# Triangle inversion in a one-core decoder-trunk kernel: the second head's products of the last four steps go to the opposite half of the partitions, and the heads get PSUM banks of their own

## The chip, the core and the metric

The kernel runs on one core of a Trainium2 chip (trn2). The core has TensorE (PE, matrix products into PSUM; its weight loads are listed apart as PEld), VectorE (DVE), ScalarE (ACT), GpSimd (POOL) and SyncE (SP, which issues most DMAs). TensorE's clock has two levels, 1.2 and 2.4 GHz, and the profile states which share of full speed was granted. The metric is the device time of one execution in microseconds (us), and lower is better.

## What is computed

One inference step of a two-layer decoder trunk: layer 0 is an RWKV-7 time mixing with a mixture of experts behind it, layer 1 a sparse attention with another mixture of experts, for a prompt of 512 tokens and 8 samples of 4 tokens. The change lies in the time mixing alone. Its recurrence runs over 16 heads of 64 channels, in f32:

```python
def wkv7_scan(r, w, k, v, a, b, s0):
    def step(s, inp):
        r_t, w_t, k_t, v_t, a_t, b_t = inp
        sa = jnp.einsum('bhij,bhj->bhi', s, a_t)
        s = s * w_t[:, :, None, :] + sa[..., None] * b_t[:, :, None, :] + v_t[..., None] * k_t[:, :, None, :]
        return s, jnp.einsum('bhij,bhj->bhi', s, r_t)
```

The kernel doesn't step through the tokens of the prompt. It cuts them into 8 chunks of 64 tokens. Within a chunk the dependence of one token on the others is a unit triangular 64x64 matrix, which has to be inverted for each head and chunk. The chunks' states are then joined one after the other.

## The kernel before

**Rounds and steps.** The heads are worked in 8 pairs (a pair is two heads, h = 0 and 1). `pe_rwkv`, `act_rwkv` and `dve_rwkv` each write out the same loop: a round per pair, a round has 8 steps s = 0 to 7, and a round works on four pairs at once: pair `a` is prepared (prep), pair `b` is inverted, pair `c` has its states computed (post, chunk), and pair `d` is finished (tail). Each engine works its own list strictly in the order of this code, and waits on semaphores for the others. On TensorE a step is the inversion of `b`, then post of `c`, then the prep of `a`, a small product for the samples, and a second prep part. So what the inversion leaves to TensorE in a step comes before everything else in that step.

**The inversion.** A pair has 16 matrices of 64x64: 2 heads, 4 values of q, and 2 values of r (chunk 2q + r). `UNITS4` lists them as (q, h, r), r fastest. An SBUF tile such as `Tt` holds the matrices with r = 0 on partitions 0 to 63 and those with r = 1 on partitions 64 to 127. `hs(r)` is that half. Steps 0 to 3 build the inverse of the 16x16 blocks by squaring. Steps 4 to 7 do two doublings (16 to 32, 32 to 64), each in two steps:
- step 4 or 6: TensorE transposes T (L958, a product with the identity) and forms L times T (L959), 2 x 16 products of 64x64x64. ScalarE copies the transposes from PSUM into `Ti` (L975), VectorE multiplies the products by a mask into `X` (L988).
- step 5 or 7: TensorE forms `Ti` times `X` (L961), 16 products. VectorE adds them to `Tt` (L991).

The tiles `X` and `Ti` are parts of the large tile `fT`, and stand under that name in the profile. Each f32 product shows as two records on TensorE, so step 4 or 6 has 64 and step 5 or 7 has 32.

**Quarters of the array.** A product of 64x64 occupies a quarter of TensorE's array: the half of its rows on whose partitions the operands lie, and the half of its columns on whose partitions the output lies. In the inversion of before, output and operands lie on the same half `p`, so all 16 products use two quarters out of four (low to low for r = 0, high to high for r = 1). Other groups of the round use all four, with one quarter after the other in the order of `UNITS4`: L1022, L1040, L865 (64 columns) and L896, L859 (128 columns).

**Other lines named below.** On TensorE: L854 transposes B and K of pair `a` (step 4), L896, L859 and L865 are its Gram products, L907 and L910 transpose the finished rows of pair `d`, L915 the incoming sample states, L1050 is the chunk recurrence of pair `c` (it waits for VectorE's L1057 each time), L872 and L873 the output gate. L951, L952 and L954 are step 0 of the inversion. On ScalarE: L1118 to L1123 copy transposed tokens, L1191 and L1192 are the tail of pair `d`. On VectorE: L1167 to L1174 and L1178, L1179 mask the Gram products of pair `a`, L1207 and L1212 belong to the tail, L1280 to the samples.

Of the kernel before, what the change touches and what calls it, by code (L numbers as in the profile page):

```python
# [7 lines left out]
ALU = mybir.AluOpType  # L8
ACT = mybir.ActivationFunctionType
# [11 lines left out]
PAIRS = 8  # L21
CH = 64
NCH = SEQ // CH
NQ = NCH // 2
# [681 lines left out]
def hs(h):  # L706
    return slice(h * HD, (h + 1) * HD)


def at(i, w=HD):  # L710
    return slice(i * w, (i + 1) * w)
# [6 lines left out]
def pe_rwkv(pe, B):  # L718

    for it in range(-1, PAIRS + 2):  # L720
        a, b, c, d = it + 1, it, it - 1, it - 2
        for s in range(8):
            if 0 <= b < PAIRS:
                pe_inverse(pe, B, b, s)
            if 0 <= c < PAIRS:
                pe_post(pe, B, c, s)
            pe_first(pe, B, a, c, d, s)
            if 0 <= b < PAIRS:
                pe_sample(pe, B, b, s)
            pe_second(pe, B, a, b, c, d, s)  # L730
            if 0 <= c < PAIRS and 3 <= s <= 5:
                pe_chunk(pe, B, c, 2 * s - 4)
            if it == PAIRS and 2 <= s <= 6:
                pe_early_rows(pe, B, s == 2, [(0, 0), (0, 4), (1, 2), (2, 0), (2, 3)][s - 2], [4, 4, 4, 3, 3][s - 2])
            if it == PAIRS + 1 and s < 4:
                pe_late_rows(pe, B, s)
# [5 lines left out]
def early_product(pe, B, q, k):  # L742

    return pe.matmul(B.bank[q][:, 0:HALF], B.wo0[q // 2][:, k, :], B.rkv[0][:, k, half(q % 2)], start=k == 0, stop=k == KT - 1)


def pe_early_rows(pe, B, first, at, count):
    S = B.sem
    if first:
        pe.wait_ge(S("pair_done"), PAIRS - 2)  # L750
        pe.wait_ge(S("inv_dve"), 7 * PAIRS)
        pe.wait_ge(S("inv_act"), 5 * PAIRS)
        pe.wait_ge(S("wo_loaded0"), 16)
        pe.wait_ge(S("wo_loaded1"), 16)
    for n in range(6 * at[0] + at[1], 6 * at[0] + at[1] + count):
        early_product(pe, B, n // 6, n % 6)
# [175 lines left out]
def pe_inverse(pe, B, b, s):  # L932
    S, bank = B.sem, B.bank
    U, L, Lp, Tt, X, Ti = B.U, B.L, B.Lp, B.Tt[b % 2], B.X, B.Ti
    if s == 0:
        pe.wait_ge(S("gram_ev"), 3 * (b + 1))
        pe.wait_ge(S("tok_ev"), 2 * (b + 1))
        if b >= 1:
            pe.wait_ge(S("inv_dve"), 7 * b)
    else:  # L940
        if s in (1, 2, 3):
            pe.wait_ge(S("inv_act"), 5 * b + s)
        if s in (5, 7):
            pe.wait_ge(S("inv_act"), 5 * b + (s + 3) // 2)
        if s >= 2:
            pe.wait_ge(S("inv_dve"), 7 * b + s - 1)
    for q, h, r in UNITS4:
        p, i = hs(r), at(h * NQ + q)
        if s <= 2:
            if s < 2:  # L950
                pe.matmul(bank[0][p, i], Lp[p, h, q], U[p, h, q], start=True, stop=True)  # L951
            mm = pe.matmul(bank[2][p, i], U[p, h, q], Lp[p, h, q], start=True, stop=True)  # L952
        if s == 0:
            mm = pe.matmul(bank[1][p, i], B.Ak[p, h, q], B.tokV[b % 2][p, q, hs(h)], start=True, stop=True)  # L954
        if s in (1, 2, 3):
            mm = pe.matmul(bank[1][p, i], Lp[p, h, q], Tt[p, h, q], start=True, stop=True)
        if s in (4, 6):
            pe.matmul(bank[0][p, i], Tt[p, h, q], B.ident[p, p], start=True, stop=True)  # L958
            mm = pe.matmul(bank[1][p, i], L[p, h, q], Tt[p, h, q], start=True, stop=True)  # L959
        if s in (5, 7):  # L960
            mm = pe.matmul(bank[2][p, i], Ti[p, h, q], X[p, h, q], start=True, stop=True)  # L961
        if q == NQ - 1 and h == 1:
            mm.then_inc(S("inv_mm"), 1)


def act_inverse(act, B, b, s):
    S, bank = B.sem, B.bank
    flat = lambda t: t.rearrange("p h q t -> p (h q t)")
    if s in (0, 1, 2, 4, 6):
        act.wait_ge(S("inv_mm"), 16 * b + 2 * s + 2)  # L970
        if s < 2:
            act.activation(flat(B.U[:]), bank[0], ACT.Copy)
        if s == 0:
            act.activation(B.AV[b % 2][:, :, :, 1, :], bank[1].rearrange("p (h q i) -> p q h i", h=2, q=NQ), ACT.Copy)
        act.activation(flat(B.Lp[:] if s <= 2 else B.Ti), bank[2 if s <= 2 else 0], ACT.Copy).then_inc(S("inv_act"), 1)  # L975


def dve_inverse(dve, B, b, s):
    S, bank = B.sem, B.bank
    quad = lambda i: bank[i].rearrange("p (h q t) -> p h q t", h=2, q=NQ)  # L980
    Tt = B.Tt[b % 2]
    if s:
        dve.wait_ge(S("inv_mm"), 16 * b + 2 * s + 2)
    if s in (1, 2, 3):
        dve.tensor_tensor(Tt[:], quad(1), Tt[:], ALU.add).then_inc(S("inv_dve"), 1)
    if s in (4, 6):
        m = B.offu[16 if s == 4 else 32]
        dve.tensor_tensor(B.X.rearrange("p h q t -> p (h q) t"), bank[1].rearrange("p (n t) -> p n t", t=CH),  # L988
                          m[:].unsqueeze(1).to_broadcast([128, 8, CH]), ALU.mult).then_inc(S("inv_dve"), 1)
    if s in (5, 7):  # L990
        dve.tensor_tensor(Tt[:], quad(2), Tt[:], ALU.add).then_inc(S("inv_dve"), 1)  # L991


def pe_post(pe, B, c, s):
    S, bank = B.sem, B.bank
    x = c % 2
    if s == 0:
        pe.wait_ge(S("inv_dve"), 7 * (c + 1))
        pe.wait_ge(S("inv_act"), 5 * c + 1)
        if c >= 1:  # L1000
            pe.wait_ge(S("post_dve"), 3 * c)
        for q, h, r in UNITS4:
            n = 2 * q + h
            mm = pe.matmul(bank[3 + n // 4][hs(r), at(n % 4, 128)], B.Tt[x][hs(r), h, q], B.AV[x][hs(r), q, h].rearrange("s k j -> s (k j)"),
                           start=True, stop=True)
            if n == 7:
                mm.then_inc(S("post_mm"), 1)
    if s == 1:
        pe.wait_ge(S("post_act"), 2 * c + 1)
        for q in range(NQ):  # L1010
            for h, r in TILES4:
                pe.matmul(bank[3 + r][hs(h), at(q)], B.WU[hs(r), q, h, 0], B.tokb[x][hs(r), q, hs(h)], start=True, stop=True)
            for h, r in TILES4:
                pe.matmul(bank[3 + r][hs(h), at(NQ + q)], B.tokk[x][hs(r), q, hs(h)], B.tokV[x][hs(r), q, hs(h)], start=True, stop=False)
            for h, r in TILES4:
                mm = pe.matmul(bank[3 + r][hs(h), at(NQ + q)], B.tokb[x][hs(r), q, hs(h)], B.WU[hs(r), q, h, 1], start=False, stop=True)
                if q == NQ - 1:
                    mm.then_inc(S("post_mm"), 1)
    if s == 2:
        pe.wait_ge(S("post_dve"), 3 * c + 1)  # L1020
        for q, h, r in UNITS4:
            mm = pe.matmul(bank[3 + r][hs(h), at(q)], B.WU[hs(r), q, h, 0], B.Rb[x][hs(r), h, q], start=True, stop=True)  # L1022
            if q == NQ - 1:
                mm.then_inc(S("post_mm"), 1)
    if s == 3:
        pe.wait_ge(S("post_dve"), 3 * c + 2)
        pe_chunk(pe, B, c, 1)
        for q, h, r in UNITS4:
            o, p = bank[4][hs(r), at(2 * q + h)], hs(r)
            pe.matmul(o, B.Rk[x][p, h, q], B.tokV[x][p, q, hs(h)], start=True, stop=False)  # L1030
            mm = pe.matmul(o, B.Rb[x][p, h, q], B.WU[p, q, h, 1], start=False, stop=True)
            if q == NQ - 1 and h == 1:
                mm.then_inc(S("post_mm"), 1)
    if 4 <= s <= 6:
        pe_chunk(pe, B, c, 2 * s - 5)
    if s == 7:
        pe.wait_ge(S("chunk_ev"), 7 * (c + 1))
        pe.wait_ge(S("post_act"), 2 * c + 2)
        for q, h, r in UNITS4:
            mm = pe.matmul(bank[3 + h][hs(r), at(q)], B.RP[hs(h), r, q], B.STh[hs(h), 2 * q + r], start=True, stop=True)  # L1040
            if q == NQ - 1:
                mm.then_inc(S("post_mm"), 1)


def pe_chunk(pe, B, c, k):
    S = B.sem
    if k >= 2:
        pe.wait_ge(S("chunk_ev"), 7 * c + k - 1)
    for h in range(2):
        pe.matmul(B.bank[3][hs(h), 0:HD], B.At[hs(h), k % 2, k // 2], B.STh[hs(h), k], start=True, stop=True).then_inc(S("chunk_mm"), 1)  # L1050
# [1970 lines left out]
```

## Time and profile before

| | |
|---|---|
| Median of 3 runs | 2147.88 us (2147.45 to 2151.01) |
| Profiled execution | 2157.4 us, its span 2155.6 us |
| Granted TensorE clock, mean | 0.925 |
| TensorE busy over the span | 1845.6 us (86%), loads 1471.2 us |
| VectorE, ScalarE busy | 688.4 us (32%), 511.9 us (24%) |
| Stretch with the inversions of the 8 pairs | 378.8 to 754.7 us |
| In 382 to 770 us: TensorE, VectorE, ScalarE busy | 321.8, 223.7, 129.4 of 388 us; clock 0.94; DMA share 0.16 |

A record of TensorE has a start and a modelled end (218 ns for 64 columns at 2.4 GHz), and records overlap. What a group of products costs is read from how far apart their starts are, or from where the next group starts, not from the sum of their durations. A pair's number is b; its round begins with step 0: pair 3 at 513.7 us, pair 4 at 569.3, pair 5 at 619.6, pair 6 at 674.9.

### The profile page before, as it was taken

What the parts mean: (1) busy time and instruction counts of PE and PEld (TensorE: products, weight loads), DVE (VectorE), ACT (ScalarE), POOL (GpSimd) and SP (SyncE); (2) the same over time, 40 slices, a digit from 0 to 9 for tenths busy, and PEclk for the clock granted to TensorE, in tenths of its full rate; (3) what the DMA queues carried; (4) which work ended last, traced back from release to release, by engine and by line L of the source; (5) the groups of instructions that cost most, each with busy time, mean ns of one, the idle gap of its engine ahead of it and who ended that gap; (6) DMA issues with size and microseconds to landing.
All of it is one profiled execution on the core that took longest, in us unless ns stands there. A gap on an engine that the chain in (4) does not pass through costs nothing.

```text
span 2155.6 us, 52984 instructions
## 1 busy us (share of the span) xinstructions
PE 1845.6 (86%) x23488; PEld 1471.2 (68%) x23488; DVE 688.4 (32%) x1810; ACT 511.9 (24%) x1115; POOL 82.4 (4%) x135
## 2 busy tenths in 40 slices
PE   5699996888888778399999699989999993999994
PEld 3476764777777656288888584468666672988883
DVE  3310023465565533311110320311777423111115
ACT  1110112333333211210010220111677512011002
POOL 2000004100000000100000100000000001000001
PEclk9799996999899989699999899989899995999997
DMA  8589826700000019589999988155000166899984
GB/s 310 174 275 293 275 91 203 229 14 13 13 13 13 9 36 323 190 315 369 373 386 356 249 167 186 53 148 136 3 2 2 38 233 239 319 372 370 372 296 149
DMA packets 184343, 409.81 MB, mean 190 GB/s; under 512 B 51350, under 2 KB 121458, under 8 KB 175890
## 3 DMA queue, kind: packets, MB, share of 16 engines
q1 hardware_dynamic: 165346, 354.26, 49.6%
q0 software_dynamic: 11040, 39.85, 5.4%
q10 hardware_dynamic: 7760, 12.79, 1.7%
q8 instruction: 158, 2.59, 0.5%
q14 instruction: 39, 0.32, 0.0%
HBM read 355.39 MB, written 55.68 MB: 191 GB/s over the span
## 4 chain that ended last, share of the span: by engine, by line
PE 67%; DVE 8%; DMA 8%; issue 7%; ACT 5%; DVEq 2%; SPq 1%; POOL 1%; ACTq 1%; POOLq 0%
PE bank L1680 9%; PE bank L413 8%; PE bank L1675 5%; PE bank L1693 4%; PE bank L1451 4%; DMA wu<-in_moe_w_up_dram 3%; PE bank L2483 3%; PE bank L1699 3%; PE bank L2532 2%; PE bank L2584 2%; PE bank L376 2%; PE bank L2621 2%; PE bank L433 1%; PE bank L1668 1%; ACT fT L631 1%
## 5 line engine op out<-in xcount | busy, mean ns | idle before, releaser
L413 PE MATMUL bank<-xm,wp 128*128 128x272 f32 x512 | 123.5, 400 | 17.8 <-DVE xm L588 17.8
L1675 PE MATMUL bank<-wg,xsT 128*32 128x384 f32 x1056 | 124.5, 509 | 9.6 <-ACT xsT L1863 4.9
L1680 PE MATMUL bank<-wg,xsT 128*32 128x128 f32 x1056 | 125.9, 282 | 0.0
L413 PEld LDWEIGHTS bank<-xm,wp 128*128 128x128 f32 x512 | 97.8, 194 | 40.8 <-DVE xm L588 18.2
L1693 PE MATMUL bank<-wd,actT 128*32 128x384 f32 x1056 | 118.0, 486 | 1.3 <-ACT actT L1876 1.3
L1680 PE MATMUL bank<-wu,xsT 128*32 128x128 f32 x1056 | 119.1, 273 | 0.0
L1680 PEld LDWEIGHTS bank<-wg,xsT 128*32 128x32 f32 x1056 | 117.8, 114 | 1.5
L1675 PE MATMUL bank<-wu,xsT 128*32 128x384 f32 x1056 | 118.5, 486 | 0.1
L1699 PE MATMUL bank<-wd,actT 128*32 128x256 f32 (+1 forms) x704 | 118.3, 326 | 0.0
L1680 PEld LDWEIGHTS bank<-wu,xsT 128*32 128x32 f32 x1056 | 115.2, 110 | 2.4
L2054 DVE COPY ys<-bank 128x384 f32<-128x384 f32 x32 | 17.9, 558 | 257.4 <-PE bank L1699 249.2
L2046 DVE TENSOR_TENSOR act<-bank,act 128x384 f32<-128x384 f32 x32 | 17.8, 558 | 245.2 <-PE bank L1680 245.2
L1699 PEld LDWEIGHTS bank<-wd,actT 128*32 128x32 f32 x704 | 76.8, 110 | 18.1
L2370 PE MATMUL bank<-region_a,fT 128*128 128x512 f32 x192 | 82.7, 593 | 0.0
L552 DVE TENSOR_TENSOR modT<-bank,vT 128x18 f32<-128x18 f32 x56 | 6.0, 170 | 204.7 <-PE bank L386 204.7
L1863 ACT ACTIVATE xsT<-bank 128x384 f32<-128x384 f32 x32 | 15.7, 491 | 220.7 <-PE bank L1668 220.7
L2370 PEld LDWEIGHTS bank<-region_a,fT 128*128 128x128 f32 x192 | 36.4, 190 | 45.7 <-issue 45.7
L952 PE MATMUL bank<-Lp,U 64*64 64x64 f32 x768 | 67.3, 227 | 0.0
L489 ACT ACTIVATE rkv<-bank 128x272 f32<-128x272 f32 x48 | 19.1, 397 | 202.8 <-PE bank L413 202.8
L2483 PE MATMUL bank<-fT,region_a 128*128 128x272 f32 x256 | 60.6, 400 | 5.5 <-issue 5.5
L376 PE MATMUL bank<-adaw,cact 128*32 128x256 f32 x816 | 54.5, 397 | 12.5 <-DMA adaw<-in_ada_w_dram 12.5
L952 PEld LDWEIGHTS bank<-Lp,U 64*64 64x64 f32 x768 | 64.8, 143 | 0.0
(566 smaller groups left out, 4195.6 us busy)
## 6 DMA issues: line engine op xcount, KB each, us to landing
wg<-in_moe_w_gate_dram SPq DMA_DIRECT2D x22, 2048.0 KB, 20.0
wu<-in_moe_w_up_dram SPq DMA_DIRECT2D x22, 2048.0 KB, 24.8
wd<-in_moe_w_down_dram SPq DMA_DIRECT2D x22, 2048.0 KB, 20.8
adaw<-in_ada_w_dram SPq DMA_DIRECT2D x43, 1024.0 KB, 8.5
w<-in_moe_w_gate_dram SPq DMA_DIRECT2D x10, 2048.0 KB, 19.8
fT<-in_moe_w_up_dram SPq DMA_DIRECT2D x10, 2048.0 KB, 24.7
gall<-in_moe_w_down_dram SPq DMA_DIRECT2D x10, 2048.0 KB, 20.3
wp<-in_rwkv_w_rkv_dram SPq DMA_DIRECT2D x24, 512.0 KB, 7.0
```

The costliest lines, as they stand in the source:

```text
L376: mm = pe.matmul(bank[4 + j % 2][32 * q:32 * q + 32, 0:256], B.cact[:, at, :], B.adab[ada_buf(u)][:, k, q * 256:(q + 1) * 256], start=at = ...
L413: mm = pe.matmul(bank[rkv_bank(n)][:, 0:HALF], B.wp[g % WP][:, k, :], B.xm[s][:, k, half(h)], start=k == 0, stop=k == KT - 1)
L952: mm = pe.matmul(bank[2][p, i], U[p, h, q], Lp[p, h, q], start=True, stop=True)
L1451: mm = pe.matmul(B.bank[q % 8][:, 0:HALF], w[k], x[:, k, half(h)], start=k == 0, stop=k == KT - 1)
L1675: mm = pe.matmul(ps[32 * j:32 * j + 32, 0:GW], B.xsT[:, k, 32 * j:32 * j + 32], w[:, k, 0:GW], start=k == 0, stop=k == KT - 1)
L1680: mm = pe.matmul(ps[96:128, q * 128:(q + 1) * 128], B.xsT[:, kk, 32 * q:32 * q + 32], w[:, kk, GW:FF], start=kk == 0, stop=kk == KT - 1)
L1693: mm = pe.matmul(bank[4 + b][32 * j:32 * j + 32, 0:384], act_piece(k, j), w[:, k, b * 384:(b + 1) * 384], start=k == 0, stop=k == 3)
L1699: mm = pe.matmul(bank[4 + b2][96:128, at:at + n], act_piece(k, q), w[:, k, col:col + n], start=k == 0, stop=k == 3)
L2370: mm = pe.matmul(bank[4 + n % 4], B.fT[:, k, cols(t)], B.wkv[:, k, c * 512:(c + 1) * 512], start=k == 0, stop=k == KT - 1)
L2483: mm = pe.matmul(bank[n % 8][:, 0:HALF], B.wq[j % 2][:, k, :], B.fT[:, k, half(h)], start=k == 0, stop=k == KT - 1)
L2532: mm = pe.matmul(bank[2 * (u % 2) + h][:, 0:128 * (i + 1)], B.qT[hs(h), j, i * 128:(i + 1) * 128], B.kT[hs(h), br, j // HG, 0:128 * (i + 1 ...
L2584: mm = pe.transpose(bank[4 + h][:, kt * 128:(kt + 1) * 128], B.sc[u % NSC][:, h, kt * 128:(kt + 1) * 128], ident[:])
```

## The change

In steps 4 to 7 the operands of a product stay on their half, and for head 1 the output goes to the other half `o = hs(r ^ h)`. Steps 4 and 6 write head 0 to banks 0 (transposes) and 1 (L times T), and head 1 to bank 2 (both, at columns 0 and 256). In `Ti` and `X` the matrices of head 1 therefore lie with r swapped. Steps 5 and 7 read them there (`Ti[o]`, `X[o]`) and write back to half p, head 0 into bank 0 and head 1 into bank 1, so `Tt` is laid out as before. The four combinations of operand half and output half now all occur.

Since bank 2 holds head 1 of both results, ScalarE and VectorE must not read it at the same time. ScalarE copies `Ti` in two halves, head 1 first. VectorE forms `X` in two halves, head 0 first, and waits for ScalarE's copy of head 1 ahead of the second. The semaphore `inv_mm` is raised by the last product of each head and r (4 per step, 2 before), in all 8 steps, and `inv_act` counts 7 per pair (5 before).

```diff
@@ pe_inverse
         if s in (5, 7):
-            pe.wait_ge(S("inv_act"), 5 * b + (s + 3) // 2)
+            pe.wait_ge(S("inv_act"), 7 * b + s)
...
     for q, h, r in UNITS4:
-        p, i = hs(r), at(h * NQ + q)
+        p, o, i, i0, i1 = hs(r), hs(r ^ h), at(h * NQ + q), at(q), at(NQ + q)
...
         if s in (4, 6):
-            pe.matmul(bank[0][p, i], Tt[p, h, q], B.ident[p, p], start=True, stop=True)
-            mm = pe.matmul(bank[1][p, i], L[p, h, q], Tt[p, h, q], start=True, stop=True)
+            pe.matmul(bank[2 * h][o, i0], Tt[p, h, q], B.ident[p, p], start=True, stop=True)
+            mm = pe.matmul(bank[1 + h][o, i1 if h else i0], L[p, h, q], Tt[p, h, q], start=True, stop=True)
         if s in (5, 7):
-            mm = pe.matmul(bank[2][p, i], Ti[p, h, q], X[p, h, q], start=True, stop=True)
-        if q == NQ - 1 and h == 1:
+            mm = pe.matmul(bank[h][p, i0], Ti[o, h, q], X[o, h, q], start=True, stop=True)
+        if q == NQ - 1:
             mm.then_inc(S("inv_mm"), 1)
@@ act_inverse
-        act.activation(flat(B.Lp[:] if s <= 2 else B.Ti), bank[2 if s <= 2 else 0], ACT.Copy).then_inc(S("inv_act"), 1)
+        if s <= 2:
+            act.activation(flat(B.Lp[:]), bank[2], ACT.Copy).then_inc(S("inv_act"), 1)
+        else:
+            for h in (1, 0):
+                act.activation(B.Ti[:, h], bank[2 * h][:, 0:256].rearrange("p (q t) -> p q t", q=NQ), ACT.Copy).then_inc(S("inv_act"), 1)
@@ dve_inverse
     if s in (4, 6):
         m = B.offu[16 if s == 4 else 32]
-        dve.tensor_tensor(B.X.rearrange("p h q t -> p (h q) t"), bank[1].rearrange("p (n t) -> p n t", t=CH),
-                          m[:].unsqueeze(1).to_broadcast([128, 8, CH]), ALU.mult).then_inc(S("inv_dve"), 1)
+        for h in range(2):
+            if h == 1:
+                dve.wait_ge(S("inv_act"), 7 * b + s)
+            ins = dve.tensor_tensor(B.X[:, h], bank[1 + h][:, 256 * h:256 * h + 256].rearrange("p (q t) -> p q t", q=NQ),
+                                    m[:].unsqueeze(1).to_broadcast([128, NQ, CH]), ALU.mult)
+        ins.then_inc(S("inv_dve"), 1)
     if s in (5, 7):
-        dve.tensor_tensor(Tt[:], quad(2), Tt[:], ALU.add).then_inc(S("inv_dve"), 1)
+        dve.tensor_tensor(Tt[:], B.ps[:, 0:2, 0:256].rearrange("p h (q t) -> p h q t", q=NQ), Tt[:], ALU.add).then_inc(S("inv_dve"), 1)
```

The waits for `inv_act` and `inv_mm` elsewhere are renumbered to match. The order of the instructions on TensorE is the same. The lines behind the change move down by 8 in the changed kernel (L1057 becomes L1065, and so on).

This is VectorE's list in steps 4 to 6 of a full round, before:

```order
178 L988 TENSOR_TENSOR fT<-bank,offu 128x512 [waits inv_mm]
179 L1057 SCALAR_TENSOR_TENSOR STh<-bank,fac,DB 128x64 [waits chunk_mm]
180 L1167 TENSOR_TENSOR U<-bank,up 128x512 [waits gram_mm]
...
193 L988 TENSOR_TENSOR fT<-bank,offu 128x512 [waits inv_mm]
194 L1057 SCALAR_TENSOR_TENSOR STh<-bank,fac,DB 128x64 [waits chunk_mm]
195 L1178 TENSOR_TENSOR L<-bank,low 128x512 [waits gram_mm]
```

And this is the same place in the changed kernel:

```order
180 L995 TENSOR_TENSOR fT<-bank,offu 128x256 [waits inv_mm]
181 L995 TENSOR_TENSOR fT<-bank,offu 128x256 [waits inv_act]
182 L1065 SCALAR_TENSOR_TENSOR STh<-bank,fac,DB 128x64 [waits chunk_mm]
183 L1175 TENSOR_TENSOR U<-bank,up 128x512 [waits gram_mm]
```

Nothing changes its place. The mask product is two instructions of 256 elements instead of one of 512, and the second of them has a wait for ScalarE.

This is ScalarE's list around step 4 and step 6, in the changed kernel (before, each couple of L979 is one L975 of 128x512):

```order
127 L979 ACTIVATE fT<-bank 128x256 [waits inv_mm]
128 L979 ACTIVATE fT<-bank 128x256
129 L1130 ACTIVATE tokk<-bank 128x512 [waits tok_mm]
130 L1131 ACTIVATE tokb<-bank 128x512
131 L979 ACTIVATE fT<-bank 128x256 [waits inv_mm]
132 L979 ACTIVATE fT<-bank 128x256
```

Both halves of `Ti` are read ahead of whatever ScalarE has next in the step.

## Rows read from the trace of the kernel before

**Rows 1.** The page: the chain that ended last, share by engine.

```profile
PE 67%; DVE 8%; DMA 8%; issue 7%; ACT 5%; DVEq 2%; SPq 1%; POOL 1%; ACTq 1%; POOLq 0%
```

**Rows 2.** Windows, the rounds of pairs 3, 4, 5: busy us, then clock, DMA share, GB/s.

```profile
513.70:569.30 55.60, 46.73 (x1026) 39.59 (x1024) 31.07 (x60) 18.82 (x32) 0.00 (x0) 0.85 0.06 13
569.30:619.60 50.30, 41.10 (x1027) 34.90 (x1026) 30.89 (x60) 18.53 (x32) 0.00 (x0) 0.99 0.07 14
619.60:674.90 55.30, 46.23 (x1027) 39.08 (x1027) 31.07 (x60) 18.92 (x32) 0.00 (x0) 0.88 0.06 13
```

**Rows 3.** Timeline of TensorE, pair 4: start, length, operation, count [idle before, releaser].

```profile
593.43 0.33 PE L958 MATMUL bank<-ident,Tt 64*64 64x64 f32 x4
...
595.56 1.09 PE L854 MATMUL bank<-ident,BK 128*128 128x128 f32 x8
...
598.86 1.11 PE L961 MATMUL bank<-fT 64*64 64x64 f32 x32
601.71 0.27 PE L1050 MATMUL bank<-STh,At 64*64 64x64 f32 x2 [1.73 <-DVE STh L1057]
...
606.55 0.33 PE L958 MATMUL bank<-ident,Tt 64*64 64x64 f32 x4
...
608.42 0.33 PE L1050 MATMUL bank<-STh,At 64*64 64x64 f32 x4
610.26 0.69 PE L865 MATMUL bank<-BK,AR 64*64 64x64 f32 x32 [1.51 <-ACT yt L1192]
...
613.09 1.08 PE L961 MATMUL bank<-fT 64*64 64x64 f32 x29
...
614.06 0.64 PE L1040 MATMUL bank<-STh,RP 64*64 64x64 f32 x30
```

**Rows 4.** Timeline of VectorE, the same round.

```profile
595.76 0.69 DVE L988 TENSOR_TENSOR fT<-bank,offu 128x512 f32<-128x512 f32 x1
...
599.07 0.69 DVE L1167 TENSOR_TENSOR U<-bank,up 128x512 f32<-128x512 f32 x1 [2.25 <-PE bank L896]
...
604.81 0.76 DVE L1212 TENSOR_TENSOR yt<-yt,rstdy 128x576 f32<-128x576 f32 x1
...
611.10 0.69 DVE L1178 TENSOR_TENSOR L<-bank,low 128x512 f32<-128x512 f32 x1 [1.36 <-PE bank L865]
```

**Rows 5.** Timeline of ScalarE, the same round.

```profile
593.87 0.59 ACT L1119 ACTIVATE AV<-bank 128x512 f32<-128x512 f32 x1
...
608.67 0.60 ACT L975 ACTIVATE fT<-bank 128x512 f32<-128x512 f32 x1 [9.29 <-PE bank L959]
609.17 0.77 ACT L1191 ACTIVATE yt<-bank,vT 128x512 f32<-128x512 f32 x1
```

**Rows 6.** Timeline of TensorE, the start of step 0 of pair 5.

```profile
619.30 0.33 PE L951 MATMUL bank<-U,Lp 64*64 64x64 f32 x2
619.47 0.22 PE L952 MATMUL bank<-Lp,U 64*64 64x64 f32 x1
619.48 0.27 PE L951 MATMUL bank<-U,Lp 64*64 64x64 f32 x1
```

**Rows 7.** Groups by line and shape, 370 to 780 us: small operations of VectorE and ScalarE.

```profile
L1263 DVE TENSOR_TENSOR GT<-bank,s_up 128x64 f32<-128x64 f32 x8 | 1.8, 219 | 7.7 <-PE bank L1239 7.7
L1292 ACT ACTIVATE stoutp<-bank 64x128 f32<-64x128 f32 x7 | 1.9, 272 | 33.8 <-PE bank L924 33.8
```

**Rows 8.** Timeline, step 6 of pairs 0 and 1, step 4 of pair 7.

```profile
411.05 0.69 DVE L1280 TENSOR_TENSOR STs<-STs,facs 128x512 f32<-128x512 f32 x1
...
455.22 0.27 PE L1050 MATMUL bank<-STh,At 64*64 64x64 f32 x2 [0.61 <-DVE STh L1057]
...
744.91 0.69 DVE L988 TENSOR_TENSOR fT<-bank,offu 128x512 f32<-128x512 f32 x1
```

**Rows 9.** Windows with L958 alone, step 6 of pair 3: PE, PEld, clock, DMA.

```profile
552.10:555.00 2.90, 2.87 (x32) 2.75 (x32) 0.63 0.02 6
```

**Rows 10.** Windows with L961 alone, step 7 of pair 3.

```profile
560.50:562.30 1.80, 1.76 (x32) 1.76 (x32) 0.50 0.00 0
```

More of the change, by code:

```diff
@@ L751, in pe_early_rows @@
         pe.wait_ge(S("inv_dve"), 7 * PAIRS)
-        pe.wait_ge(S("inv_act"), 5 * PAIRS)
+        pe.wait_ge(S("inv_act"), 7 * PAIRS)
         pe.wait_ge(S("wo_loaded0"), 16)
@@ L941, in pe_inverse @@
         if s in (1, 2, 3):
-            pe.wait_ge(S("inv_act"), 5 * b + s)
+            pe.wait_ge(S("inv_act"), 7 * b + s)
         if s in (5, 7):
-            pe.wait_ge(S("inv_act"), 5 * b + (s + 3) // 2)
+            pe.wait_ge(S("inv_act"), 7 * b + s)
         if s >= 2:
@@ L969, in act_inverse @@
     if s in (0, 1, 2, 4, 6):
-        act.wait_ge(S("inv_mm"), 16 * b + 2 * s + 2)
+        act.wait_ge(S("inv_mm"), 32 * b + 4 * s + 4)
         if s < 2:
@@ L982, in dve_inverse @@
     if s:
-        dve.wait_ge(S("inv_mm"), 16 * b + 2 * s + 2)
+        dve.wait_ge(S("inv_mm"), 32 * b + 4 * s + 4)
     if s in (1, 2, 3):
@@ L998, in pe_post @@
         pe.wait_ge(S("inv_dve"), 7 * (c + 1))
-        pe.wait_ge(S("inv_act"), 5 * c + 1)
+        pe.wait_ge(S("inv_act"), 7 * c + 1)
         if c >= 1:
```

## The prediction

> **What bounds the kernel now.** I read the chain that ended last first. TensorE holds 67% of it, VectorE 8% and ScalarE 5% [rows 1], so time taken from TensorE may count, but only where it stands on the chain of its round. I then cut the time mixing into rounds. The rounds of pairs 3, 4 and 5 take 55.6, 50.3 and 55.3 us for the same work (1026 or 1027 matmul records each), and the difference goes with the granted clock: 0.85, 0.99, 0.88 [rows 2]. So a round costs about 50.3 us, and 5.15 us more (the mean of 55.6 and 55.3, less 50.3) where TensorE falls from 2.4 to 1.2 GHz in part of it. DMA is at 6 or 7% there and plays no part. Last I followed one round, pair 4, through steps 4 to 7 on the three engines.
>
> How fast do the inversion's products go? Step 6 runs from 606.55 to the start of L1050 at 608.42 [rows 3]: 64 records in 1.87 us, 29.2 ns each. In step 5 the 32 records of L961 take 1.11 us with the last one's length of 0.22 in it: (1.11 - 0.22) / 31 = 28.7 ns. Now the groups that go round all four quarters of the array: L865, with the same 64x64 products, takes 0.69 us for 32 records, (0.69 - 0.22) / 31 = 15.2 ns, and L1040 (0.64 - 0.22) / 29 = 14.5 ns [rows 3]. With two quarters a record costs twice what it does with four. That is the effect the change is after, and this trace has the price on both sides.
>
> **Step by step.** I take 15.2 ns, the dearer of the two. Steps 4 and 6 go from 1.87 to 64 x 15.2 = 0.97 us, a saving of 0.90 each. Steps 5 and 7 save 32 x (28.7 - 15.2) = 0.43 each. What of this is on the chain:
> - Step 4: TensorE goes straight from the inversion through L1050 to L854, which starts at 595.56. L854 also needs ScalarE's L1119, which ends at 593.87 + 0.59 = 594.46 [rows 5]. The inversion would end at 593.43 + 0.97 = 594.40, and L1050 comes between, so the cover just suffices and L854 moves by the full 0.90. What hangs on it follows: ScalarE's token copies, L896, and VectorE's L1167, which waited 2.25 us for L896 [rows 4]. VectorE's mask product L988 isn't bound by TensorE here (595.76, behind the tail), and has over a second microsecond of room before L1167. Pairs 0 to 6: 7 x 0.90 = 6.3 us. Pair 7 has no prep, and there L988 starts at 744.91 [rows 8], behind VectorE's own work and not at the inversion's end, so nothing is saved.
> - Step 5: TensorE ends L961 and then stands 1.73 us until VectorE's L1057 [rows 3], because VectorE works without a break from 599.07 (L1167) to L1212 at 604.81 [rows 4]. The 0.43 goes into this wait: 0.
> - Step 6: behind the inversion come ScalarE's copy (608.67), L1191 (609.17), L1192, and L865 at 610.26, which waited 1.51 us for the latter [rows 3, 5]. All of it moves forward. Pairs 2 to 6 save 0.90 less the dearer copy (below, 0.07): 5 x 0.83 = 4.15. Pair 7 saves 0.90 less the dearer mask product (0.15), 0.75. Pairs 0 and 1 have no tail. There VectorE's L1280 runs from 411.05 to 411.74, and L1050 and L865 wait for VectorE's L1057 until 455.22 [rows 8], so I count 0. Sum 4.9.
> - Step 7: L915, then L961 from 613.09, then L1040 at 614.06 and the gate products, with no wait on TensorE between [rows 3]. All 8 pairs: 8 x 0.43 = 3.4.
> - At 1.2 GHz the same products cost double. Pair 3's step 6 takes 2.90 us at a clock of 0.63, and its step 7 1.80 at 0.50 [rows 9, 10]. Half of the surplus over 1.87 goes as well, 0.5, and another 0.43 in step 7. Pairs 2, 3 and 5 are like that: 3 x 0.93 = 2.8. Sum of gains: 6.3 + 4.9 + 3.4 + 2.8 = 17.4 us.
>
> **The costs.** A VectorE product of 64 elements takes 0.219 us [rows 7] and one of 512 takes 0.69 [rows 4]: 1.05 ns an element, so 0.42 for 256, and 0.84 for two with a wait between, against 0.69: 0.15 more (bounds: 0 and 0.69, two full ones). It is hidden in step 4 and in step 6 of pairs 2 to 6, since L1167 and L1178 wait for TensorE for over a microsecond. It counts at pairs 0 and 1 in step 6 and at pair 7 in step 4: 0.45. Behind the waiting half stand L1057 and the next L1050. The half of ScalarE's copy that it waits for is the first of two, 0.38 us by 0.272 for 128 and 0.60 for 512 elements [rows 5, 7], so it is ready by the time that VectorE's first half is. ScalarE starts L1191 0.50 after the start of a copy of 0.60, so two of 0.38 hold it for 2 x 0.28 = 0.56: 0.07 with rounding, already taken off.
>
> The signal is dearer too. The last record of step 6 starts ahead of 608.42 and ends by 608.64, and ScalarE starts at 608.67: 0.03 later, with 2 increments in the group. L865 ends at 610.26 + 0.69 = 610.95 and L1178 starts at 611.10: 0.15 later, with 4 increments [rows 3 to 5]. So I charge 0.10 at the 6 hand-overs of step 6 that count, 0.6. The added increments of steps 0 to 3 are bounded by 0 and by 32 x 0.05 = 1.6 (half the surplus, since nothing else changes there). TensorE has other work behind most of these, and I take 0.4. The Trainium skill, "TensorE: Matmul & The Clock Gate", section "The cost: per-tile semaphore tail", speaks against such increments: they are written one after another at 26 ns each. By that rule alone two more in each of 64 steps are at most 3.4 us, against my 1.0. The trace's 0.15 against 0.03 agrees in sign and is larger.
>
> Net: 17.4 - 0.45 - 0.6 - 0.4 = 16.0 us (15.95) of the profiled 2157.4. That execution is 9.5 us above the median of the runs shown, which may be two cold rounds more; I take the 16.0 off the median: 2147.9 - 16.0 = **2131.9 us**, 0.74% faster.
>
> **The rivals.** *The run of four records.* In L865 a quarter gets 2 records before the next quarter's turn, in steps 4 and 6 it gets 4 (transpose and product of one matrix), and no group in this trace has four records a turn over four quarters. If the queue can't look past a full quarter, steps 4 and 6 stay at 29.2 ns. What speaks against it is step 0, with six records a turn on two quarters: the second quarter's first L951 starts at 619.48, right behind the third record of the first (L952, 619.47), while three records of the first quarter are still to start [rows 6]. So three can wait in front of a busy quarter, and a turn of four (one running, three waiting) blocks nobody. Then only step 7 gains: 3.4 + 1.3 (cold) - 0.7 = 4.0 us, **2143.9**. The Trainium skill, same page, "The mechanism", says that matmuls start and end strictly in program order. By that rule this rival would be certain. The trace disagrees, since at 619.48 a later product starts ahead of three earlier ones.
>
> *The shared bank.* Banks 0, 1 and 2 each take output from both operand halves, where L865 and L1040 give each operand half a bank of its own. If such writes took turns, nothing would be gained and the costs of 1.5 remain with halves of it hidden: **2148.6**. The Trainium skill, "TensorEngine Tiling (Array Packing)", "Gotcha 1: PSUM Pressure", states that row tiles can't use one bank at the same time. Against it: before, both operand halves already write into bank 0 or 1, and 29.2 ns a record is 58.4 a quarter, the same as the 4 x 14.5 = 58 of L1040 [rows 3]. Nothing is taking turns.
>
> *The clock, the other sign.* The change takes TensorE's work out of the very stretch ahead of which it sometimes falls to 1.2 GHz. Round 3 fell in step 6, behind VectorE's long run, and round 4 with the same work didn't. If a thinner TensorE let further rounds fall, each costs 5.15 less 0.93 (the cold gain), 4.2 us. Four more balance the gain, and from five on the kernel is slower. With all six that are warm now: 6 x 4.2 - 16.0 = 9.3, **2157.2**. What speaks against it: the work is the same and only packed tighter, so a stretch with step 6 in it holds more, not less. It may as well go the other way. *Rounds 3 and 5 stay warm*: 16.0 - 1.9 + 10.3 = 24.4, **2123.5**.
>
> **How the numbers follow.** Forecast 0.70 (with its own range 2126 to 2138: one cold round more or less, and the costs at either bound), run of four 0.12, shared bank 0.04, clock lost 0.04, clock kept 0.10. The range **2122 to 2144** leaves out the shared bank, the lost clock and some of the edges, under 2 in 10. A difference of 0.2% (4.3 us, below 2143.6) is about what can be told from no change. Faster: 0.70 + 0.10 + half of 0.12 = 0.86. Same: 0.06 + 0.04 = 0.10. Slower: 0.04.
>
> **What would show it.** In the changed profile, step 4 and step 6 should take about 0.97 us at full clock, L961 0.69 for 32 records, and L854 should start 0.9 sooner after the first L958. TensorE's wait ahead of L1050 in step 5 should grow from 1.73 to about 2.1. L865 should follow the end of step 6 by some 1.8 instead of 1.6. A warm round should take 50.3 - 0.90 - 0.73 - 0.43 = 48.2 us. I'm wrong if step 6 stays near 1.87 (run of four or bank), if L854 now waits for L1119, or if the clock of the rounds moves: that alone is worth 5 us a round, more than any other term.

## The result and the profile after

The changed kernel took 2167.64 us (median of 4 runs, 2162.91 to 2170.04), the kernel before 2147.77 us (4 runs, 2147.45 to 2151.01). The ratio of the mean times is 1.0086 with a 95% interval of 1.007 to 1.0103: 0.86% slower, where 0.74% faster was forecast. The profiled execution took 2167.08 us with a span of 2165.3 and a mean granted clock of 0.905, against 0.925 before.

The page of the changed kernel, chain that ended last, by engine (it answers to [rows 1]):

```profile
PE 69%; DVE 8%; DMA 8%; issue 7%; ACT 5%; DVEq 2%; POOL 1%; SPq 1%; ACTq 1%; POOLq 0%
```

TensorE's share went up by two points although its products got faster. Below, a round or stretch is called warm where TensorE has its full clock, and cold where it is at 1.2 GHz in part of it. A fall is a change from 2.4 to 1.2 GHz. The rounds of pairs 3 to 6 show where, by windows (busy us of PE, PEld, DVE, ACT, POOL; then the clock, the DMA share, GB/s):

```profile
511.20:569.00 57.80, 49.18 (x1026) 39.56 (x1025) 31.30 (x62) 18.80 (x34) 0.00 (x0) 0.77 0.06 12
569.00:627.20 58.20, 49.52 (x1026) 39.88 (x1025) 31.38 (x62) 18.79 (x34) 0.00 (x0) 0.76 0.06 12
627.20:685.00 57.80, 49.19 (x1026) 39.52 (x1025) 31.29 (x62) 18.78 (x34) 0.00 (x0) 0.77 0.06 12
685.00:742.90 57.90, 49.16 (x1026) 39.50 (x1025) 31.29 (x62) 18.80 (x34) 0.00 (x0) 0.77 0.06 12
```

Against [rows 2], each of these rounds is now cold, and colder than the cold ones of before: a clock of 0.77 where it was 0.85 to 0.99. These four rounds take 231.7 us. Before, they ran from 513.7 to 725.3, which is 211.6. The 20.1 us between them are as much as the difference of the medians (19.9), but this match is in part chance. The two profiled executions differ by 9.7 us only: the one of before lies 9.6 us above its median and ran 10.4 us longer outside these rounds (2.5 ahead of them, 7.9 behind them).

Did the shortened steps shorten? TensorE's timeline in the round of pair 4, and in step 6 of pair 2, the last one that met full clock (it answers to [rows 3]):

```profile
494.76 0.33 PE L958 MATMUL bank<-ident,Tt 64*64 64x64 f32 x6
494.88 0.22 PE L959 MATMUL bank<-Tt,L 64*64 64x64 f32 x1
494.89 0.23 PE L958 MATMUL bank<-ident,Tt 64*64 64x64 f32 x2
...
497.72 0.69 PE L865 MATMUL bank<-BK,AR 64*64 64x64 f32 x32 [1.69 <-ACT yt L1200]
...
596.77 0.33 PE L958 MATMUL bank<-ident,Tt 64*64 64x64 f32 x6
...
597.92 0.33 PE L1058 MATMUL bank<-STh,At 64*64 64x64 f32 x4
598.18 1.09 PE L854 MATMUL bank<-ident,BK 128*128 128x128 f32 x8
...
601.49 0.65 PE L961 MATMUL bank<-fT 64*64 64x64 f32 x30
604.34 0.27 PE L1058 MATMUL bank<-STh,At 64*64 64x64 f32 x2 [2.20 <-DVE STh L1065]
...
608.45 1.09 PE L907 MATMUL bank<-ident,yt 128*128 128x128 f32 x4 [0.84 <-DVE yt L1220]
```

They did. Step 4 runs from 596.77 to L1058 at 597.92, 1.15 us for 64 records, 18 ns each, against 29.2. L854 follows the first L958 by 1.41 us instead of 2.13. From the first L958 of step 6 to L865 it is 2.96 us at full clock, against 3.71 [rows 3]. L961 takes (0.65 - 0.22) / 29 = 15 ns a record. The wait ahead of the chunk product of step 5 grew from 1.73 to 2.20. So the products gained most of what was asked of them, and the time was lost elsewhere.

Windows over the round of pair 4, cut where the clock changes, show where:

```profile
597.00:601.60 4.60, 3.81 (x129) 3.41 (x125) 2.88 (x7) 3.73 (x7) 0.00 (x0) 1.00 0.02 5
601.60:605.00 3.40, 1.20 (x61) 1.06 (x56) 3.03 (x6) 0.40 (x2) 0.00 (x0) 1.00 0.00 0
605.00:611.90 6.90, 6.06 (x104) 4.08 (x94) 4.69 (x10) 0.00 (x0) 0.00 (x0) 0.51 0.01 2
611.90:615.30 3.40, 1.13 (x48) 0.85 (x41) 1.86 (x5) 1.59 (x4) 0.00 (x0) 1.00 0.00 0
615.30:629.00 13.70, 12.21 (x131) 8.42 (x133) 3.52 (x7) 1.88 (x3) 0.00 (x0) 0.50 0.02 4
629.00:635.80 6.80, 6.30 (x150) 5.50 (x146) 0.06 (x1) 4.69 (x7) 0.00 (x0) 1.00 0.40 80
635.80:642.60 6.80, 6.80 (x90) 5.86 (x91) 4.68 (x10) 2.10 (x3) 0.00 (x0) 0.50 0.01 2
```

There are three stretches at 1.2 GHz, 27.4 us in all, where pair 4's round of before had a mean clock of 0.99 [rows 2]. The first is entered behind 601.6 to 605.0, where TensorE is busy for 1.20 of 3.40 us because L961 is done early and the chunk product waits for VectorE. The second and longest is entered behind 611.9 to 615.3 (1.13 of 3.40), the wait for ScalarE between the end of step 6 and L865, and the one ahead of L915. It then covers the gate products of step 7 and the next round's step 0, where TensorE has few waits to absorb it: L872 and L873 start 1.20 us apart, against 0.66 before. The third meets steps 0 and 1.

How much emptier did these stretches get? Here are the same places in pair 4's round of before (step 5, then the end of step 6), where no fall followed; then step 5 of pair 2 in the changed kernel, where none followed either; and last the stretch ahead of the third fall:

```profile
598.96:602.36 3.40, 1.67 (x62) 1.53 (x61) 3.01 (x6) 0.41 (x2) 0.00 (x0) 1.00 0.02 5
608.50:611.90 3.40, 1.21 (x49) 0.93 (x43) 1.77 (x4) 1.54 (x3) 0.00 (x0) 1.00 0.00 0
...
487.18:490.58 3.40, 1.20 (x61) 1.06 (x56) 3.02 (x6) 0.41 (x2) 0.00 (x0) 1.00 0.03 5
632.40:635.80 3.40, 2.90 (x61) 2.12 (x57) 0.06 (x1) 3.20 (x5) 0.00 (x0) 0.99 0.02 3
```

The stretch of step 5 has less work than before (1.67 to 1.20), the one behind step 6 hardly less (1.21 to 1.13). The same 1.20 brought a fall in pair 4 and none in pair 2, and the third fall came behind 2.90. TensorE's busy time just ahead does not by itself tell where the clock falls.

### The profile page after: what moved, and what is told of

Same layout as the page of the kernel before. It is cut to its first block, busy times and chain, and to the rows that moved or that the text cites. A ratio compares the mean times of both kernels' runs of the same rounds, so it can differ in the third digit from the quotient of the medians.

```text
span 2165.3 us, 53016 instructions
## 1 busy us (share of the span) xinstructions
PE 1862.4 (86%) x23488; PEld 1473.8 (68%) x23488; DVE 690.9 (32%) x1826; ACT 512.6 (24%) x1131; POOL 82.1 (4%) x135
## 4 chain that ended last, share of the span: by engine, by line
PE 69%; DVE 8%; DMA 8%; issue 7%; ACT 5%; DVEq 2%; POOL 1%; SPq 1%; ACTq 1%; POOLq 0%
PE bank L1688 9%; PE bank L413 8%; PE bank L1683 5%; PE bank L1459 4%; PE bank L1701 4%; DMA wu<-in_moe_w_up_dram 3%; PE bank L2491 3%; PE bank L1707 3%; PE bank L2540 2%; PE bank L2592 2%; PE bank L376 2%; PE bank L2629 2%; PE bank L433 1%; PE bank L951 1%; PE bank L1676 1%
## 5 line engine op out<-in xcount | busy, mean ns | idle before, releaser
L952 PE MATMUL bank<-Lp,U 64*64 64x64 f32 x768 | 78.7, 246 | 0.0
L952 PEld LDWEIGHTS bank<-Lp,U 64*64 64x64 f32 x768 | 75.2, 162 | 0.0
L951 PEld LDWEIGHTS bank<-U,Lp 64*64 64x64 f32 x512 | 60.4, 171 | 7.4 <-issue 6.6
L951 PE MATMUL bank<-U,Lp 64*64 64x64 f32 x512 | 64.7, 266 | 0.7 <-ACT STs L1134 0.7
```

## The experiments

Each was timed beside the kernel before on its own chip, where that kernel's median was 2151.8 us (first four), 2152.5 us (next four) and 2152.0 us (last three), so the ratios are what compares. Each profile is of one execution, and not always of one near the median. Below, "all fillers" are products whose results nobody reads, put in front of TensorE's waits:

```diff
+def pe_fill(pe, B, n):
+    for i in range(n):
+        pe.matmul(B.bank[4][:, 0:256], B.ident[:], B.wa2[:, 256 * (i % 4):256 * (i % 4) + 256], start=True, stop=True)
...
+            full = 0 <= c and a < PAIRS
             if 0 <= b < PAIRS:
                 pe_inverse(pe, B, b, s)
+            if full and s == 5:
+                pe.wait_ge(S("post_act"), 2 * c + 2)
+                pe_fill(pe, B, 3)
             if 0 <= c < PAIRS:
                 pe_post(pe, B, c, s)
+            if full and s == 6:
+                pe_fill(pe, B, 3)
             pe_first(pe, B, a, c, d, s)
             if 0 <= b < PAIRS:
                 pe_sample(pe, B, b, s)
+            if full and s in (5, 6):
+                pe_fill(pe, B, 3 if s == 5 else 2)
             pe_second(pe, B, a, b, c, d, s)
```

**The change with all fillers.**

> The changed kernel, with products that compute nothing needed (128x128 by 128x256, output to bank 4 while it is free) put in front of TensorE's waits in steps 5 and 6: 3 ahead of the chunk product of step 5, 3 ahead of the tail transposes of step 5, 3 ahead of L865's wait, 2 ahead of the state transposes, in rounds 1 to 6. Each is about 0.43 us at 2.4 GHz, so they fit into waits of 2.2, 1.9, 1.5 and 1.2 us. Clock theory (the shortened steps let TensorE fall to 1.2 GHz in every round from 3 on, and a cold round is 58 us against 48.2 warm): the fillers keep the clock, rounds go to 48 to 49 us, total 2110 to 2125 us. Cost theory (split copies, the new wait, the added increments lengthen the rounds themselves): no gain, 2167 to 2175 us.

2119.78 us (4 runs, 2117.68 to 2122.09), ratio 0.9865 (0.9848 to 0.9883). This is 1.35% faster than the kernel before, with the change untouched and work added. Windows over its rounds of pairs 3 to 5:

```profile
508.50:556.40 47.90, 43.61 (x1050) 35.72 (x1049) 31.07 (x62) 18.87 (x34) 0.00 (x0) 1.00 0.07 15
556.40:604.40 48.00, 43.71 (x1047) 35.79 (x1045) 31.08 (x62) 18.75 (x34) 0.00 (x0) 1.00 0.07 15
604.40:652.20 47.80, 43.51 (x1047) 35.62 (x1047) 31.07 (x62) 18.77 (x34) 0.00 (x0) 1.00 0.07 15
```

The clock is 1.00 in all of them and a round takes 47.9 us, 10 less than without fillers. TensorE's timeline shows the fillers (L721) in place, in step 6 of pair 4, and the end of that round:

```profile
593.78 1.56 PE L721 MATMUL bank<-wa,ident 128*128 128x256 f32 x6
595.54 0.69 PE L881 MATMUL bank<-BK,AR 64*64 64x64 f32 x32 [0.20 <-ACT yt L1216]
...
597.73 0.71 PE L931 MATMUL bank<-ident,stio 64*128 64x64 f32 x8 [0.16 <-DVE Lp L1203]
598.37 0.69 PE L977 MATMUL bank<-fT 64*64 64x64 f32 x32
598.88 0.65 PE L1064 MATMUL bank<-STh,RP 64*64 64x64 f32 x32
599.46 0.73 PE L888 MATMUL bank<-hg,g 128*128 128x272 f32 x2
```

The wait ahead of the Gram product (L865, here L881) is 0.20 us instead of 1.69. It still starts when ScalarE is ready, so the fillers cost nothing on the chain. Step 7's stretch from L915 to L872 is 2.18 us in the kernel before; here, as L931 to L888, it runs from 597.73 to 599.46, 1.73 us. The 0.45 are the forecast's 0.43. The rows of before:

```profile
612.45 0.71 PE L915 MATMUL bank<-ident,stio 64*128 64x64 f32 x8 [1.22 <-DVE Lp L1179]
...
614.63 0.72 PE L872 MATMUL bank<-hg,g 128*128 128x272 f32 x2
```

**The kernel before with all fillers.**

> The kernel before with the same fillers in the same four places. Clock theory: its two cold rounds (3 and 5, 5.2 us each) go to 50.3 us and smaller falls go too, total 2132 to 2140 us, and the distance to the changed kernel with fillers is the change's own worth, 14 to 18 us. If fillers only cost time: 2148 to 2155 us.

2155.03 us (10 runs, 2147.03 to 2162.16), ratio 1.0024 (1.0006 to 1.0041). The expected gain didn't come. So the change alone costs 0.86%, the fillers alone 0.24%, and both together gain 1.35%. In its profile (its fastest run, 2147.03) the falls of steps 6 and 7 are gone, but some in steps 0 and 1 remain, where there is no filler. Windows: the rounds of pairs 2 to 5, then the stretch ahead of a fall in step 0 of pair 4's round, and that fall:

```profile
464.50:513.90 49.40, 46.28 (x1048) 38.46 (x1047) 30.96 (x60) 17.41 (x31) 0.00 (x0) 1.00 0.07 14
513.90:563.90 50.00, 46.35 (x1048) 38.46 (x1047) 30.87 (x60) 18.70 (x32) 0.00 (x0) 1.00 0.07 14
563.90:615.40 51.50, 47.87 (x1047) 39.64 (x1047) 30.96 (x60) 18.67 (x32) 0.00 (x0) 0.97 0.07 14
615.40:668.50 53.10, 49.47 (x1049) 41.14 (x1049) 30.96 (x60) 18.71 (x32) 0.00 (x0) 0.94 0.06 13
...
568.90:572.30 3.40, 2.90 (x59) 2.23 (x58) 0.55 (x2) 3.35 (x4) 0.00 (x0) 1.00 0.19 44
572.30:575.70 3.40, 3.40 (x46) 2.70 (x46) 3.23 (x7) 1.55 (x2) 0.00 (x0) 0.50 0.00 0
```

This fall too came behind 2.90 of 3.40 us of busy TensorE. In the changed kernel with all fillers the same part of step 0 has the same share and no fall:

```profile
563.20:566.60 3.40, 2.90 (x63) 2.36 (x62) 2.32 (x3) 2.67 (x5) 0.00 (x0) 1.00 0.00 0
```

Two rounds are wholly at full clock, 49.4 (pair 2) and 50.0 us (pair 3). With the change they are 47.2 and 47.9. That is the change's own worth at equal clock: 2.1 to 2.2 us a round, where the forecast's terms gave 0.90 + 0.83 + 0.43 less the hand-over's 0.10, 2.06. The medians of the two kernels with fillers are 35 us apart, more than this in eight rounds. The rest is presumably rounds of before that stay cold.

**All banks, splits and waits, but the same half.**

```diff
-        p, o, i, i0, i1 = hs(r), hs(r ^ h), at(h * NQ + q), at(q), at(NQ + q)
+        p, o, i, i0, i1 = hs(r), hs(r), at(h * NQ + q), at(q), at(NQ + q)
```

> The changed kernel with all its banks, split copies, waits and increments, but head 1's output left on the operands' own half: two quarters of the array as before, 29 ns a record. Clock theory: TensorE's load is that of before, 2147 to 2152 us (the costs of the split alone, 1.5 us). Cost theory: 2165 us or more, since everything that it blames is still there.

2156.98 us (10 runs, 2144.21 to 2161.44), ratio 1.0014 (0.999 to 1.0038): no difference from before that can be told, though the median lies above the expected 2147 to 2152 and costs of up to 0.38% are not excluded. Its rounds of pairs 3 and 4:

```profile
514.10:564.50 50.40, 41.15 (x1025) 34.95 (x1024) 31.07 (x62) 18.60 (x34) 0.00 (x0) 0.99 0.07 13
564.50:619.80 55.30, 46.17 (x1027) 39.03 (x1026) 31.27 (x62) 19.02 (x34) 0.00 (x0) 0.88 0.06 13
```

This is the pattern of before within 0.1 us [rows 2], shifted by a round. So the split copies, VectorE's wait and the added increments are not what costs the 0.86%. The opposite half is, and it is the part that is faster.

**The opposite half in steps 6 and 7 only, and in steps 4 and 5 only.**

```diff
-        p, o, i, i0, i1 = hs(r), hs(r ^ h), at(h * NQ + q), at(q), at(NQ + q)
+        p, o, i, i0, i1 = hs(r), hs(r ^ h if s >= 6 else r), at(h * NQ + q), at(q), at(NQ + q)
```

> The changed kernel with the opposite half used in steps 6 and 7 only; steps 4 and 5 are on the operands' own half, with the same split and waits. Clock theory: step 6 is where the clock falls, so most rounds from 3 on should be cold at 57 to 59 us, 2160 to 2170 us. If the fall comes from the sum of both places or from when the round meets it, fewer rounds are cold, 2140 to 2160 us. Cost theory: the same as with the same half everywhere.

The other kernel has `s <= 5` in place of `s >= 6`:

> The changed kernel with the opposite half used in steps 4 and 5 only; steps 6 and 7 stay on the operands' own half. Clock theory: steps 6 and 7 keep TensorE as loaded behind VectorE's long run as before, so the clock falls in fewer rounds than with steps 6 and 7 alone (55 to 57 us a round there), 50 to 55 us a round, 2140 to 2158 us. If it is the shorter step 4 and 5 ahead of that run that starve the clock, rounds are 55 us or more and the time is 2158 us or more.

Steps 6 and 7: 2160.17 us, ratio 1.005 (1.0032 to 1.0069), its profiled rounds of pairs 3 to 6 at 57.0, 55.0, 55.2 and 57.0 us with a clock of 0.83 to 0.87. Steps 4 and 5: 2150.55 us, ratio 0.9982 (0.9958 to 1.0006), rounds of 55.6, 54.6, 50.3 and 55.6 us at 0.85 to 0.96. Of these four rounds, all are cold with the part in steps 6 and 7 and three with the part in steps 4 and 5, where two were cold before. The part in steps 6 and 7 loses by it; the part in steps 4 and 5 comes out even.

**Fillers in step 5 only, and in step 6 only.** The change with six of the eleven fillers of a round, and with the other five:

> The changed kernel with the fillers of step 5 alone (3 ahead of the chunk product, 3 ahead of the tail transposes). In the changed kernel a round has two falls in steps 5 to 7: one from inside step 5 on, one from step 6 on. Clock theory: the first fall goes, the second (behind the end of step 6) may stay; rounds 50 to 55 us, 2125 to 2150 us. If the first fall is what brings the second, rounds are 48 us and the time is that of all fillers, 2117 to 2123 us.

> The changed kernel with the fillers of step 6 alone (3 ahead of L865's wait, 2 ahead of the state transposes). Clock theory: the fall from step 6 on goes and the one inside step 5 may stay; rounds 50 to 54 us, 2125 to 2150 us. Here a filler met at 1.2 GHz takes 0.86 us and three overrun the wait of 1.5 us, so a round that is cold in step 6 could also pay 1 us for them.

Step 5 only: 2147.53 us (10 runs, 2136.42 to 2152.26), ratio 0.9981 (0.9957 to 1.0005). Step 6 only: 2127.72 us (4 runs, 2122.3 to 2132.93), ratio 0.9887 (0.9844 to 0.993). One window over steps 6 to 0 in the former, and the round of pair 6 in the latter:

```profile
604.50:618.20 13.70, 12.63 (x138) 8.88 (x140) 3.10 (x7) 1.88 (x3) 0.00 (x0) 0.50 0.04 7
```

```profile
657.30:705.10 47.80, 40.52 (x1035) 33.53 (x1033) 31.10 (x62) 18.75 (x34) 0.00 (x0) 1.00 0.07 15
```

With step 5 filled, the long stretch at 1.2 GHz behind step 6 is still there in full in the round shown; in the other profiled rounds the cold stretches there are shorter. With step 6 filled the long stretch is gone in all profiled rounds (47.6 to 51.5 us). By the medians, the fillers of step 5 alone take back 20 us, those of step 6 alone 40, and all of them 48. So most of the loss hangs on TensorE's waits in step 6, between the end of the inversion and step 7, and a part on those of step 5. The interval of step 6 alone overlaps that of all fillers (0.9848 to 0.9883), so the two are not told apart.

**The same instructions without the work.** All fillers in their places, each of them 32x32 by 32x8:

```diff
-        pe.matmul(B.bank[4][:, 0:256], B.ident[:], B.wa2[:, 256 * (i % 4):256 * (i % 4) + 256], start=True, stop=True)
+        pe.matmul(B.bank[4][0:32, 0:8], B.ident[0:32, 0:32], B.wa2[0:32, 8 * i:8 * i + 8], start=True, stop=True)
```

> The changed kernel with the same number of products in the same four places as with all fillers, but each only 32x32 by 32x8: the instructions, their place and the added wait without the work. Clock theory: the clock needs work, not instructions, so rounds stay at 57 to 59 us and the time at 2163 to 2172 us. If the break in the queue or a shift in time is what helped, it comes down to 2120 to 2140 us.

2165.94 us (7 runs, 2158.45 to 2171.81), ratio 1.0063 (1.0036 to 1.009). The last two of its rounds before pair 7:

```profile
621.40:679.40 58.00, 50.42 (x1048) 40.70 (x1048) 31.29 (x62) 18.82 (x34) 0.00 (x0) 0.76 0.06 12
679.40:737.40 58.00, 50.42 (x1048) 40.71 (x1047) 31.29 (x62) 18.81 (x34) 0.00 (x0) 0.76 0.06 12
```

There are as many records as with full fillers (1048), and these rounds are as cold as with none. The three before them (52.6, 53.5 and 54.2 us, at 0.84 to 0.85) are cold too, but less so: the profile is of the fastest of the seven runs. The wait for `post_act`, the break in the queue and the added instructions thus bring no gain. The work in the fillers does it.

**More, shifted and less.** Three variants of all fillers: one more filler ahead of L896 in step 4 and two ahead of L924 in step 7 (bank 2); one more in step 4 right behind the inversion, where it lies on the chain; and 2, 2, 2, 1 instead of 3, 3, 3, 2.

> The changed kernel with all fillers of steps 5 and 6, and also 1 filler ahead of L896's wait in step 4 (0.79 us) and 2 ahead of L924's wait in step 7 (0.89 us, output to bank 2, which is free there). Clock theory: rounds 1 to 6 were warm already with the first fillers (47.8 us), so there is little left to win: 2112 to 2122 us. If the last two fillers overrun their wait, 1 to 3 us are lost, up to 2124 us.

> The changed kernel with all fillers of steps 5 and 6, and 1 more filler (0.43 us at 2.4 GHz) in step 4 behind the inversion, where TensorE goes on without a wait, so that it lies on the chain of rounds 1 to 6. If rounds are sums of their parts, the total grows by 6 x 0.43 = 2.6 us to 2121 to 2125 us. If warm rounds depend on where in time they fall, the shift of each round by 0.43 us brings falls back and costs much more, 2128 us and above.

> The changed kernel with one product less in each of the four places (2, 2, 2 and 1 instead of 3, 3, 3 and 2). Clock theory: the work in the waits is what counts, so with 7 of 11 products some rounds fall again, between all fillers and none: 2122 to 2145 us. If the dose was more than enough, it stays at 2117 to 2123 us.

More: 2128.91 us (6 runs, 2119.53 to 2138.63), ratio 0.9884 (0.9851 to 0.9916). On the chain: 2131.6 us (2127.5 to 2136.46), ratio 0.9901 (0.9876 to 0.9927). Less: 2134.45 us (2121.49 to 2139.98), ratio 0.9896 (0.9863 to 0.9928). The rounds of pairs 3 and 4 of the second, and then its step 4 in pair 3's round, from the first product of the inversion (L976) over the filler (L721) to the transposes of B and K (L854 of before, here L872):

```profile
511.90:561.60 49.70, 45.40 (x1052) 36.77 (x1051) 31.10 (x62) 19.08 (x34) 0.00 (x0) 0.98 0.07 15
561.60:614.00 52.40, 48.12 (x1050) 39.33 (x1049) 31.19 (x62) 18.58 (x34) 0.00 (x0) 0.92 0.06 13
...
535.76 0.33 PE L976 MATMUL bank<-ident,Tt 64*64 64x64 f32 x6
...
536.94 0.70 PE L721 MATMUL bank<-wa,ident 128*128 128x256 f32 x2
...
537.84 1.09 PE L872 MATMUL bank<-ident,BK 128*128 128x128 f32 x8
```

From the first product to these transposes it is 2.08 us, against 1.41 without the filler: one product on the chain costs 0.67 us a round, not the 0.43 that was reckoned. The rounds of pairs 3 and 4 are longer by 1.8 and 4.4 us (47.9 and 48.0 with all fillers), since falls come back. With six times 0.67 the sum would be 2123.8 us, and the median is 2131.6. More work in more waits did not help either: its profiled rounds of pairs 4 to 6 have a clock of 0.93 and take 50.9 to 51.1 us, with a fall in steps 0 and 1, where no filler stands:

```profile
562.80:569.60 6.80, 6.66 (x87) 5.71 (x89) 4.74 (x10) 2.28 (x4) 0.00 (x0) 0.50 0.01 2
```

The falls in the rounds of pairs 3 to 5 with less filler lie in the same place. None of the three is better than the first set, but none is told from it with certainty either: the interval of each ratio overlaps 0.9848 to 0.9883, and the three profiles are each of the slowest of six runs. They suggest that it is not a plain matter of how much filler there is, and that where a round stands in time matters as well; this is not shown.

## Why the prediction was wrong

**The rate held, nearly.** "With two quarters a record costs twice what it does with four": it is 18 ns in step 4 and 15 in steps 5 and 7, against the 15.2 used. Step 4 saved 0.72 and not 0.90: the term was 0.18 too large. From the start of step 6 to L865 0.75 was saved (forecast, with copy and hand-over taken off, 0.73), in step 7 0.45 (0.43). The three add up to 1.92, and where the rest of the 2.1 to 2.2 of a warm round lies was not looked for. Why step 4 is a little slower than 15 ns a record is not shown; the run of four records on a quarter is one candidate. Both rate rivals fell. The queue does look past a busy quarter: in the rows from 494.76 on, six records of L958 start ahead of the first of L959, where program order has two of each in turn. And the shared bank does not take turns, with the two operand halves in opposite partition halves of it. The Trainium skill's rules named there, on program order and on row tiles and banks, do not describe this case, since the forecast reckoned that either would hold step 4 at 1.87 us, and it took 1.15.

**The hidden steps were read rightly.** The 0.43 of step 5 went into the wait, 1.73 to 2.20. VectorE's two half products took 0.76 together where 0.84 was counted, and ScalarE's L1199 starts 0.55 us behind its first half copy where 0.56 was counted. The hand-over of step 6, charged with 0.10 more, shows 0.02 more: in pair 2 ScalarE's copy starts at 496.07, 0.05 behind the end of the last record of L959 at 496.02, where it was 0.03. The same-half experiment bounds all those costs together only loosely: 0.14%, with an interval from -0.10 to 0.38%. In one small place the working does not agree with itself: it counts pairs 2, 3 and 5 as cold, which leaves five warm rounds and not the six of the rival of the lost clock, 2152.9 us instead of 2157.2.

**The step that failed** is the clock. The sum gives it no term, so it takes as many cold rounds after the change as before, and the rival that had it otherwise was dismissed with a reason: "the work is the same and only packed tighter, so a stretch with step 6 in it holds more, not less". The stretches behind which the clock fell in steps 5 to 7 are not those with step 6 in them but the ones around the waits. There the change takes work out: 1.20 us of TensorE instead of 1.67 in 3.40 in step 5, and 1.13 instead of 1.21 behind the end of step 6, and the waits are longer (2.20 instead of 1.73, and 1.65 to 1.69 instead of 1.51). I gave this 0.04, and priced it too low as well. A cold round was put at 5.15 us more than a warm one, from [rows 2]. In the changed kernel it is 57.9 - 47.9 = 10.0 us (the warm round being that of the kernel with fillers), because the clock falls three times in a round, and the longest stretch covers the gate products and step 0. The forecast for that rival, 2157.2, was in turn 10 us short.

**The sum that stands.** In the rounds of pairs 3 to 6 the profiles give it as follows. With fillers and at full clock these rounds take 191.6 us with the change; without the change I put them at 4 x 50.0 = 200.0, by the round of pair 3, an estimate. So the change is worth 8.4 us there. Cold stretches cost 211.6 - 200.0 = 11.6 us before and 231.7 - 191.6 = 40.1 us after, 28.5 more. The difference, 20.1, is the loss.

**What is shown and what is not.** Three things are shown. The loss needs the opposite half (same half). It goes away with work in TensorE's waits of steps 5 and 6, and not with the same instructions without work (all fillers against tiny ones). Step 6 carries the larger part of it (step 6 only against step 5 only). The Trainium skill, "TensorE: Matmul & The Clock Gate", section "HAM oscillation — how this bites in real kernels", says that idle time between bursts lowers the clock and that each following burst pays. The trace agrees in kind for two of the three falls, behind stretches with 1.20 and 1.13 us of TensorE in 3.40. It does not for the third, behind 2.90. What decides whether a given round falls stays open. Pair 2's round of the changed kernel went through steps 4 to 6 warm and the next four did not, with the same instructions and the same 1.20 us in step 5. It also stays open why the same fillers did nothing for the kernel before.

## What to carry to other kernels

Where a group of small products can use all four quarters of TensorE's array, it may run faster, here by 1.6 times in step 4 and 1.9 times in step 7. But TensorE's clock can take back more than that if the group stands beside waits, as it did here. Before making TensorE faster, mark in the trace where it waits and where its clock has fallen already. Here two of four equal rounds were cold before the change, and they belonged in the sum as its largest uncertain term. A cheap test is a few unread products in front of the waits, into a bank that is free, beside the same number of tiny ones. Put them into the kernel before as well: here they gained 1.35% with the change and nothing without it, so they are no remedy to rely on.

## What the runs showed of the hardware that was not expected

- In several profiles rounds repeat, by themselves or in turns: 57.8, 58.2, 57.8, 57.9 us in the changed kernel, 47.9, 48.0, 47.8, 47.9 with fillers, and 50.4, 55.3, 50.5, 55.7 in turn with the same half. A kernel with equal rounds seems to settle into a pattern with its falls. With a shift of 0.67 us a round, single rounds were up to 4.4 us longer.
- The clock fell behind stretches with 1.13, 1.20 and 2.90 us of busy TensorE in 3.40, and did not fall behind others with 1.20, 1.21 and 2.90.
- The added increments, put at 1.0 us in all, are too small to be seen in any timed comparison here. At the one hand-over that was read they show as 0.02 us.
- The kernel before, timed on another chip, spread from 2141.88 to 2162.06 us over 22 runs, against 2147.45 to 2151.01 in the first four. Its shortest run had a mean clock of 0.929, its longest 0.921, so where the clock falls seems to be a source of scatter too.
